# Two neighbouring weight rows in one partition: expert weights as 8 KB packets in a two-layer mixture-of-experts trunk

## What is computed

```python
def expert_choice_ffn(h, router, w_gate, w_up, w_down):
    cap = EC_CAPACITY * n // N_EXPERTS
    aff = jax.nn.softmax((h @ router).astype(F32), axis=-1)
    gate, idx = lax.top_k(jnp.swapaxes(aff, 1, 2), cap)
    def per_request(hb, gb, ib):
        xe = hb[ib]
        a = jnp.einsum('ecd,edf->ecf', xe, w_gate)
        b = jnp.einsum('ecd,edf->ecf', xe, w_up)
        ye = jnp.einsum('ecf,efd->ecd', jax.nn.silu(a) * b, w_down) * gb[..., None]
        return jnp.zeros_like(hb).at[ib.reshape(-1)].add(ye.reshape(-1, d))
...
h2 = rms_norm(x, lw['norm2_g']) * (1 + sc2) + sh2
x = x + g2 * expert_choice_ffn(h2, lw['router'], lw['w_gate'], lw['w_up'], lw['w_down'])
```

## Time and profile before

| | us |
|---|---|
| median of 3 runs (lowest, highest) | 2083.75 (2082.91, 2087.36) |
| span of the profiled execution, first to last instruction | 2081.3 |
| TensorE busy in it | 1946.8 (94%) |
| expert loop of layer 0, first L1238 to end of the last L1282 | 502.3 to 1046.7 |
| expert loop of layer 1, the same | 1518.0 to 2061.6 |

### The profile page before, as it was taken

How to read it: one execution, slowest core, us unless ns; L and a number is a source line. 1 busy time by engine, 2 the same in 40 slices (tenths; PEclk the granted TensorE clock), 3 DMA queues, 4 the chain that set the end, 5 groups by cost and what they waited for, 6 DMA issues and landing times.

```text
span 2081.3 us, 36417 instructions
## 1 busy us (share of the span) xinstructions
PE 1946.8 (94%) x14936; PEld 1084.3 (52%) x14936; DVE 533.9 (26%) x1187; ACT 450.5 (22%) x947; POOL 160.5 (8%) x140
## 2 busy tenths in 40 slices
PE   4999999996999999999989999989699999999996
PEld 3756677882444434343365657778544344434342
DVE  1157123533101111111131932253511111111013
ACT  3132232221211111121132214332221121212112
POOL 0000001100111010101000000020010101111110
PEclk8999999996999999999999999999799999999998
DMA  8313122347999999999934122214559999999996
GB/s 311 102 43 122 41 82 85 115 169 271 381 385 395 388 390 393 389 394 390 398 132 139 41 83 81 81 62 194 214 211 392 390 393 389 394 386 397 385 397 240
DMA packets 172887, 532.98 MB, mean 256 GB/s; under 512 B 17296, under 2 KB 50192, under 8 KB 172560
## 3 DMA queue, kind: packets, MB, share of 16 engines
q1 hardware_dynamic: 155248, 493.53, 61.5%
q0 software_dynamic: 11712, 22.29, 4.9%
q10 hardware_dynamic: 5856, 16.16, 2.0%
HBM read 506.59 MB, written 25.33 MB: 256 GB/s over the span
## 4 chain that ended last, share of the span: by engine, by line
PE 66%; DMA 15%; SPq 9%; DVE 5%; issue 4%; ACT 1%; DVEq 0%; ACTq 0%
PE wide L1238 12%; DMA ring<-w_up 12%; PE wide L837 9%; PE wide L827 8%; SPq L644 7%; PE wide L1118 6%; PE wide L1246 6%; PE narrow L1269 6%; PE wide L1282 3%; DMA ring<-w_down 2%; PE turned L786 2%; PE narrow L758 1%; PE wide L954 1%; DMA ring<-w_mod 1%; PE narrow L990 1%
## 5 line engine op out<-in xcount | busy, mean ns | idle before, releaser
L1238 PE MATMUL wide<-ring,ht 128*64 128x512 f32 x2048 | 454.1, 599 | 9.4 <-DMA ring<-w_up 4.8
L1238 PEld LDWEIGHTS wide<-ring,ht 128*64 128x64 f32 x2048 | 143.6, 138 | 304.6 <-issue 278.3
L1269 PE MATMUL narrow<-ring,ht 128*64 128x512 f32 x1024 | 234.3, 599 | 2.3 <-DMA ring<-w_down 2.3
L1246 PE MATMUL wide<-ring,ht 128*32 128x256 f32 x4096 | 234.3, 380 | 0.0
L2202 DVE TENSOR_TENSOR ht<-ht,wide 128x512 f32<-128x512 f32 x64 | 35.5, 555 | 679.6 <-ACT ht L1760 459.2
L837 PE MATMUL wide<-stream,ht 128*128 128x256 f32 (+1 forms) x960 | 195.2, 365 | 3.5 <-DVE ht L1861 3.5
L837 PEld LDWEIGHTS wide<-stream,ht 128*128 128x128 f32 x960 | 171.3, 192 | 26.0 <-issue 5.0
L1246 PEld LDWEIGHTS wide<-ring,ht 128*32 128x32 f32 x4096 | 126.5, 110 | 108.2 <-issue 31.3
L827 PE MATMUL wide<-ht,stream 128*128 128x128 f32 (+1 forms) x640 | 176.3, 437 | 0.0
L1760 ACT ACTIVATE ht<-wide 128x512 f32<-128x512 f32 x32 | 19.1, 597 | 622.7 <-PE wide L1238 622.7
L2408 POOL DMA_INDIRECT moe_sums<-ht x60 | 93.3, 1554 | 712.2 <-DVE ht L2219 637.0
(11 more groups left out here) (283 smaller groups left out, 1549.9 us busy)
## 6 DMA issues: line engine op xcount, KB each, us to landing
ring<-w_gate SPq DMA_DIRECT2D x256, 512.0 KB, 12.3
ring<-w_up SPq DMA_DIRECT2D x256, 512.0 KB, 14.2
ring<-w_down SPq DMA_DIRECT2D x128, 1024.0 KB, 19.9
stream<-w_mod SPq DMA_DIRECT2D x38, 1024.0 KB, 5.4
stream<-w_in SPq DMA_DIRECT2D x20, 1024.0 KB, 7.4
ring<-w_mod SPq DMA_DIRECT2D x10, 1024.0 KB, 18.8
stream<-w_out SPq DMA_DIRECT2D x6, 1024.0 KB, 7.4
moe_sums<-x ACTq DMA_DIRECT2D x10, 512.0 KB, 5.5
```

What stands on the lines that cost most here:

```text
L1238: ins = mm(psW[h * 64:(h + 1) * 64, 0, w * HALFW:(w + 1) * HALFW], xT[:, k, 0:CAPS], ring[:, k, w, h * HALFW:(h + 1) * HALFW], start=(k == ...
L1246: ins = mm(psW[q * STRIP:(q + 1) * STRIP, 1, w * QW:(w + 1) * QW], xT[:, k, CAPS:SLOTS], ring[:, k, w, q * QW:(q + 1) * QW], start=(k == 0 ...
L1269: ins = mm(psN[c * 64:(c + 1) * 64, 0, :], hmT[:, j, h_ * 64:(h_ + 1) * 64], ring[:, KD + k // 2, k % 2, c * HALFW:(c + 1) * HALFW], start ...
```

## The change

A gate or up transfer takes 256 successive rows, and partition p gets rows 2p and 2p + 1 of them: 8192 contiguous bytes in HBM and in the partition. One DMA of 1 MB fills one slot; slot 2i holds chunks 2i and 2i + 1 of gate, slot 2i + 1 those of up. w_down lands in the same manner. Chunk k of a contraction is now every second row of a block of 256, so the transposes that make the other operand read every second column (`paired`), and modulation groups 3 and 4, `norm2_g` and the router follow on the host or in `mod_columns`. Waits and releases of gate and up slots go by pairs of chunks. An expert takes 12 DMAs for 20.

```diff
+PAIRED_GROUPS = (3, 4)
...
+        def paired(v, k):
+            return v.rearrange("p (c n r) -> p c r n", n=P, r=2)[:, k // 2, k % 2, :]
...
             def load_head(l, u):
                 slot = u - NSTREAM
-                sp.wait_ge(s_gu_used, l * EXPERTS * KD + slot + 1)
+                sp.wait_ge(s_gu_used, l * EXPERTS * KD + 2 * (slot // 2) + 2)
...
-            def load_gateup(l, e, k):
-                for i, w in enumerate(("w_gate", "w_up")):
-                    src = io[w][bass.ds(l, 1), bass.ds(e, 1), k * P:(k + 1) * P, :]
-                    sp.dma_start(ring[:, k, i, :], src.rearrange("l e p n -> (l e p) n")).then_inc(s_slot[k], 16)
-
-            def load_down(l, e, j):
-                src = down_h[bass.ds(l, 1), bass.ds(e, 1), :, 2 * j:2 * j + 2, :]
-                sp.dma_start(ring[:, KD + j, :, :], src.rearrange("l e p k n -> (l e p) k n")).then_inc(s_slot[KD + j], 16)
-
             def load_slot(l, e, slot):
-                if slot < KD:
-                    load_gateup(l, e, slot)
-                else:
-                    load_down(l, e, slot - KD)
+                weights, pair = (io[("w_gate", "w_up")[slot % 2]], slot // 2) if slot < KD else (io["w_down"], slot - KD)
+                src = weights[bass.ds(l, 1), bass.ds(e, 1), 2 * P * pair:2 * P * (pair + 1), :]
+                sp.dma_start(ring[:, slot].rearrange("p r n -> p (r n)"), src.rearrange("l e (p r) n -> (l e p) (r n)", r=2)).then_inc(s_slot[slot], 16)
...
                 with sp.Fori(1, EXPERTS) as e:
-                    for k in range(KD):
-
-                        sp.wait_ge(s_gu_used, (l * EXPERTS + e) * KD + k + 1)
+                    for pair in range(KD // 2):
+
+                        sp.wait_ge(s_gu_used, (l * EXPERTS + e) * KD + 2 * pair + 2)
                         settle(sp)
-                        load_gateup(l, e, k)
+                        load_slot(l, e, 2 * pair)
+                        load_slot(l, e, 2 * pair + 1)
                     for j in range(4):
                         sp.wait_ge(s_dn_used, (l * EXPERTS + e) * 4 + j - 3)
                         settle(sp)
-                        load_down(l, e, j)
+                        load_slot(l, e, KD + j)
...
+                    cols = paired(mod_rows[:, g % 2, :], b) if g in PAIRED_GROUPS else mod_rows[:, g % 2, b * P:(b + 1) * P]
...
-                transposes(l, f"xt.{t}.{half}", [(o[:, j * P:(j + 1) * P], x[:, t, (4 * half + j) * P:(4 * half + j + 1) * P]) for j in range(4)])
+                transposes(l, f"xt.{t}.{half}", [(o[:, j * P:(j + 1) * P], paired(x[:, t, :], 4 * half + j)) for j in range(4)])
...
-                        ins = nc.tensor.transpose(bank(T, job)[:, k * GROWS:(k + 1) * GROWS], rows[:, (4 * i + k) * P:(4 * i + k + 1) * P], ident[0:GROWS, 0:GROWS])
+                        ins = nc.tensor.transpose(bank(T, job)[:, k * GROWS:(k + 1) * GROWS], paired(rows, 4 * i + k), ident[0:GROWS, 0:GROWS])
...
+            def gate_up(k, w):
+                return ring[:, k - k % 2 + w, k % 2, :]
+
             def latent_gate_up(m):
                 for k in range(KD):
-                    pe.wait_ge(s_slot[k], (m + 1) * 32)
+                    if k % 2 == 0:
+                        for w in range(2):
+                            pe.wait_ge(s_slot[k + w], (m + 1) * 16)
...
-                    ins = nc.tensor.transpose(dst[:, j * P:(j + 1) * P], src[:, j * P:(j + 1) * P], ident)
+                    ins = nc.tensor.transpose(dst[:, j * P:(j + 1) * P], paired(src, j), ident)
```

More of the change, by code:

```diff
@@ L551, in build @@
         out_h = io["w_out"].rearrange("l (k p) n -> l p k n", p=P)
-        down_h = io["w_down"].rearrange("l e (k p) n -> l e p k n", p=P)
         block = ctx.enter_context(nc.Block())
@@ L773, in mod_columns @@
                 for b in range(NG):
-                    ins = mm(o.rearrange("p (q b c) -> p b q c", q=PARTS, b=NG)[:, b], mod_rows[:, g % 2, b * P:(b + 1) * P],
+                    cols = paired(mod_rows[:, g % 2, :], b) if g in PAIRED_GROUPS else mod_rows[:, g % 2, b * P:(b + 1) * P]
+                    ins = mm(o.rearrange("p (q b c) -> p b q c", q=PARTS, b=NG)[:, b], cols,
                              con("strips").rearrange("p (q c) -> p q c", q=PARTS), start=False, stop=(b == NG - 1))
@@ L1228, in turn_rows_in @@
                     for k in range(4):
-                        ins = nc.tensor.transpose(bank(T, job)[:, k * GROWS:(k + 1) * GROWS], rows[:, (4 * i + k) * P:(4 * i + k + 1) * P], ident[0:GROWS, 0:GROWS])
+                        ins = nc.tensor.transpose(bank(T, job)[:, k * GROWS:(k + 1) * GROWS], paired(rows, 4 * i + k), ident[0:GROWS, 0:GROWS])
                     T.finish(ins)
+            def gate_up(k, w):
+                return ring[:, k - k % 2 + w, k % 2, :]
             def latent_gate_up(m):
                 for k in range(KD):
-                    pe.wait_ge(s_slot[k], (m + 1) * 32)
+                    if k % 2 == 0:
+                        for w in range(2):
+                            pe.wait_ge(s_slot[k + w], (m + 1) * 16)
                     for w in range(2):
                         for h in range(2):
-                            ins = mm(psW[h * 64:(h + 1) * 64, 0, w * HALFW:(w + 1) * HALFW], xT[:, k, 0:CAPS], ring[:, k, w, h * HALFW:(h + 1) * HALFW], start=(k == 0), stop=(k == KD - 1))
+                            ins = mm(psW[h * 64:(h + 1) * 64, 0, w * HALFW:(w + 1) * HALFW], xT[:, k, 0:CAPS], gate_up(k, w)[:, h * HALFW:(h + 1) * HALFW], start=(k == 0), stop=(k == KD - 1))
                 ins.then_inc(s_lat_up, 1)
@@ L1246, in context_gate_up @@
                             ins = mm(psW[q * STRIP:(q + 1) * STRIP, 1, w * QW:(w + 1) * QW], xT[:, k, CAPS:SLOTS],
-                                     ring[:, k, w, q * QW:(q + 1) * QW], start=(k == 0 and w == 0), stop=(k == KD - 1 and w == 1))
+                                     gate_up(k, w)[:, q * QW:(q + 1) * QW], start=(k == 0 and w == 0), stop=(k == KD - 1 and w == 1))
                     ins.then_inc(s_gu_used, 1)
@@ L2485, in everywhere, with paired_columns @@
         return np.repeat(v.reshape(DEPTH, 1, -1), P, axis=1)
-    for name, key in (("n1g", "norm1_g"), ("n2g", "norm2_g"), ("bmod", "b_mod"), ("sgg", "sg_norm_g"), ("convb", "conv_b"),
+    def paired_columns(v):
+        return v.reshape(DEPTH, -1, P, 2).transpose(0, 2, 1, 3)
+    put("n2g", paired_columns(a["norm2_g"]))
+    for name, key in (("n1g", "norm1_g"), ("bmod", "b_mod"), ("sgg", "sg_norm_g"), ("convb", "conv_b"),
                       ("lng", "conv_ln_g"), ("lnb", "conv_ln_b"), ("gng", "ret_gn_g")):
         put(name, columns(a[key]))
+    for g in PAIRED_GROUPS:
+        put("bmod", paired_columns(a["b_mod"][:, g * D:(g + 1) * D]), cols=(KD * g, KD * (g + 1)))
     rt = np.zeros((DEPTH, P, KD, STRIP), np.float32)
-    rt[..., 0:EXPERTS] = a["router"].reshape(DEPTH, KD, P, EXPERTS).transpose(0, 2, 1, 3)
+    rt[..., 0:EXPERTS] = a["router"].reshape(DEPTH, KD // 2, P, 2, EXPERTS).transpose(0, 2, 1, 3, 4).reshape(DEPTH, P, KD, EXPERTS)
     put("router", rt)
```

## The result

The change makes the kernel slower: 2101.15 us median of four runs (2094.09 to 2103.52) against 2083.33 of the kernel before beside it, a ratio of 1.0080 with a 95% interval of 1.0064 to 1.0095. The forecast was 2080.0, the range 2071.5 to 2090.

The account below looks back on a forecast made before the run. DMA was taken to bound the expert loops, 34.01 us an expert against TensorE's 33.49. From 2083.75, less 11.3 for packets, plus 7.5 for later loop heads, with strided transposes at nothing, came 2080.0 us; range 2071.5 to 2090.

Parts of the forecast that it names:

- Part 1: Expert loops of both layers: 8 KB packets take 314 to 317 ns, DMA stops binding, all 11.3 us of weight waits go.
- Rival 2: Expert loops: 8 KB packets no cheaper, loop stays at DMA's 34.01 us, heads still later: 2091.2 us; chance 0.15.
- rival 4: Weight loads: packets are cut into 4 KB again, only the steps change: about 2084 us; chance 0.05.
- Part 2: Gate and up slots: waits and releases in pairs cost nothing; without cover, at most 0.9 us an expert.
- Part 3: Transposes loading with a step of two floats: taken as nothing, upper end 2.0 us an expert, 63 us in all.
- the heads: Start of each layer's expert loop: the store of rows and first gather come later, 7.5 us in sum.
- rival 3: Transposes: strided loads cost their upper end or a third of it: 2100 to 2143 us; chance 0.06.
- Part 4: Loop heads: queues take turns by packets, so the store lands 4.5 and 2.3 us later; 7.5 with the gather's 0.7.
- Rival 1: Loop heads: queues share by bytes, or the store gets through otherwise; no delay, 2072.4 us; chance 0.20.
- The in-loop gather: Expert loop: adds and gathers at most 3.3 us later, hidden by nearly 4 us spare.
- rival 5: Expert loop: the gather's spare 4 us are used up, each expert waits for rows, some us slower; chance 0.04.

## Why the prediction was wrong, point by point

**Part 1 (packets): right.** 8192 B take 311 ns, just under the 314 to 317 forecast. The loop is no longer bound by DMA, and with contiguous turns the two loops are 10.9 us shorter, for 11.3. The Trainium skill's limit for such loads (DMA: Bandwidth & Descriptors, "Where 436 GB/s comes from", about 358 GB/s) does not hold here, with one core at work: 427 GB/s in 760:775. Rival 2 is out. So is rival 4: of the 877 packets there 781 are of 8 KB, the others under 512 B.

**Part 2 (coarser steps): right.** With pair steps and contiguous turns the experts are 33.49 us apart and no wait for a slot is in the chain.

**Part 3 (strided turns): the step that failed.** It was taken at nothing; it is 0.57 us an expert, some 18 us in all, as much as the packets and the heads together could have given or taken. The mechanism stood as rival 3 ("their upper end or a third of it: 2100 to 2143"), and the lower of its two ends is where the time fell. That is partly luck: no row stood behind the third, 21 us, where 18 were measured, and the heads added 2.2 more than forecast. But it got 0.06, because "nothing but the missing row speaks for it". Two things were wrong in that. The reason given, the same number of elements from the same partitions, counts what is read and not how; and the nearest row was chosen among turns only, where the trace of before also had loads of 128 columns for plain matmuls:

```profile
L837 PEld LDWEIGHTS wide<-stream,ht 128*128 128x128 f32 x960 | 171.3, 192 | 26.0 <-issue 5.0
...
L1229 PEld LDWEIGHTS turned<-const_cols,xn_yt 80*128 80x128 f32 x256 | 20.2, 144 | 18.3 <-issue 18.3
```

(groups of before, mean ns after the comma). Two loads of 128 columns that differ by 48 ns say that 141 is the quick case, and that a load of another form may well fall to 190. At 48 ns for each of 14 turns that is an estimate of 0.7 us an expert; 0.57 was measured. It would also have shown at once that there was no room: the shortage to be removed was only 0.52 us an expert (DMA's 34.01 over TensorE's 33.49), so any price above that makes the loop as slow as it had been, and the first seven experts slower too. The 40 turns a layer after the output projection, the other place of the step, hardly mattered: their loads went from 141 to 205 ns as well, but TensorE's busy time in them only from 10.7 to 11.6 us in all.

The sentence from the Trainium skill (SBUF — State Buffer, "Door 1: The DMA port swizzle"), by which two hits to a 16-byte line run at full rate, agrees with plain loads (195 and 201 ns) and not with a transpose's (141 and 223). Nor do the turns follow that rule: steps of 4 and 8, one hit to a line at most, take 286 and 278 ns, a step of two 283.

**Part 4 (queues take turns): right in kind, 2.2 us small.** The store is 4.0 and 2.3 us later for 4.5 and 2.3. What was mis-sized is the gather itself. In layer 0 it now falls among the parameters' rows of 14.2 KB, as foreseen, but from issue to the first turn it takes 10.7 us for 8.4: 2.3 later where 0.7 was taken. One DMA queue in 492:498, after and then before, shows its company, 10.6 KB a packet for 3.8:

```profile
q1 hardware_dynamic: 123, 1.30, 72.2%
```

```profile
q1 hardware_dynamic: 480, 1.84, 84.6%
```

Another 0.9 is TensorE having finished earlier. Rival 1 (by bytes, no delay) is out: with 4 KB packets the delay is gone, and without expert weights beside it the store takes 9.9 us for 22.7. This agrees with the Trainium skill (DMA: Bandwidth & Descriptors, "Queues, rings and completion order") that an engine goes round its queues by packets. A packet in the Trainium skill's sense there is a bundle of descriptors, typically some 9 to 17; whether the queues take turns by single rows or by such bundles, the counts here don't tell.

**The in-loop gather: right.** GpSimd's wait for an expert's adds grows from 6.8 to about 9 us, and no wait of TensorE for rows appears in the loop; rival 5 is out.

**The sum.** Without Part 3 it was good: 2080.0 forecast, 2080.29 measured with contiguous turns. By the ratio, 0.9994, that kernel is 1.2 us under the kernel before where the forecast had 3.8; the interval holds both. (In the forecast's first part 5.6 + 5.8 should be 5.5 + 5.8; the 11.3 is right.) The forecast's error is one term, put at zero with its upper end known, and given a chance that didn't fit how little was known of it.

## What to carry to other kernels

Price a new access pattern of the bound engine by every row that does the same work in another form, not by the row that looks most alike: two forms of one load at 141 and 190 ns are the warning that a third may not be at 141. When a change lifts one limit by little (0.52 us an expert here), first ask what it adds to the next limit: 14 turns at 40 ns more each use all of it up. Where a layout in memory dictates an order, look for an engine with time to spare to make it (ACT and DVE did it here at no price that the loop shows) rather than the one that sets the time.

## What the runs showed that was not expected

- A transpose's stationary load of 128 contiguous f32 columns takes 141 ns; with a step of 2, 4 or 8 floats some 195 to 223; in the same turns as plain matmuls it takes 190 to 195, and 196 to 201 with a step of two.
- The turn's own price is smaller than the load's: 50 ns a turn of rows (244 to 294) and 25 ns a hidden turn (292 to 317) for some 65 to 80 ns of load. The loads of successive turns overlap: eight in a row take 0.62 us contiguous, where eight times 141 ns would be 1.13, and 1.03 with the step of two (timelines of loads, the changed kernel with contiguous turns first, then the changed kernel). The 0.41 us between them is what the eight turns lost.

```profile
562.27 0.62 PEld L1226 LDWEIGHTS turned<-const_cols,xn_yt 80*128 80x128 f32 x8 [0.41 <-issue]
```

```profile
559.04 1.03 PEld L1226 LDWEIGHTS turned<-const_cols,xn_yt 80*128 80x128 f32 x8 [0.41 <-issue]
```

- ACT and DVE read PSUM with a step of two floats at no extra time (597 and 688 ns for 128x512); ACT's read of SBUF in that order costs 1222 ns for 1136 (128x1024).
- Two limits of one loop don't add: with 4 KB packets (11 us of waits in the kernel before) and strided turns (18 us) it is 7 us above the kernel before, not 18.
